# Powers in smaller pieces, two low parts and the phase tables later, and twelve rounds of transposes at other pairs, in a two-block transformer kernel

## The reference

```python
def first_block(x, ...):
    for layer in range(2):
        u_ssm, u_g, v_g, q, k, v = split(rms_norm(h, g) @ w_in[layer])
        mixed = concatenate([s5_mixer(u_ssm, ...), spatial_gating(u_g, v_g, ...), diff_attention(q, k, v, ...)])
        h = h + mixed @ w_out[layer]
        h = h + conv_gated_mlp(rms_norm(h, g2), w_up[layer], conv_w, conv_b, w_down[layer])   # 1024 -> 2 x 2816 -> 1024

def s5_mixer(u, ...):      # a complex diagonal state space model in 16 groups, 64 states each
    a_bar = exp(lam * dt); b_bar = ((a_bar - 1) / lam) * b
    states = associative_scan(...)            # s[t] = a_bar * s[t-1] + b_bar u[t]
    y = real(c @ states) + d_skip * u         # then GELU and a gated linear unit

def conv_gated_mlp(x, ...):
    h = x @ w_up
    acc = conv_b + conv_w[0] * h[t-2] + conv_w[1] * h[t-1] + conv_w[2] * h[t]
    gate, val = split(acc);  return (gelu(gate) * val) @ w_down

def second_block(x, mem, ...):
    a_qkv, bq, bk, bv, mq, ga, gb, gm, mg = split(rms_norm(x, g) @ w_in)
    # branch a: three dilated window attentions over rotated queries and keys
    # branch b: attention with normed, rotated heads; branch m: attention over 256 memory rows
    # the three branches are gated, projected, merged, projected and normed
```

## Time and profile before

| | us |
|---|---|
| Runs of the kernel | 999.23, 1001.0, 1001.94 (median 1001.0) |
| The profiled execution | 999.57 |
| Its span | 997.8 |
| TensorE busy | 966.1 |
| VectorE busy | 701.2 |
| ScalarE busy | 547.1 |
| GpSimd busy | 252.9 |

### The profile page before, as it was taken

One profiled execution on the slowest core, in us unless ns is written; L12 is line 12 of the kernel. 1 busy time (PEld: TensorE's weight loads), 2 busy tenths in 40 slices (PEclk: granted clock), 3 DMA queues, 4 the chain that ended last, 5 costly groups with the idle time before them and its releaser, 6 DMA issues.

```text
span 997.8 us, 15915 instructions
## 1 busy us (share of the span) xinstructions
PE 966.1 (97%) x6214; PEld 848.8 (85%) x6214; DVE 701.2 (70%) x1072; ACT 547.1 (55%) x898; POOL 252.9 (25%) x196
## 2 busy tenths in 40 slices
PE   6989999999999999999999999999999999999997
PEld 4868789999888887889999988999877789888886
DVE  6998557798954688657677856547676755666785
ACT  7645546665654655645576545545354454555723
POOL 4890102688400021102525300003112300000030
PEclk9999999999999999999999999999999999999999
DMA  7622355655565553247666664665544545754462
GB/s 295 213 84 85 88 186 178 189 179 177 172 188 166 168 171 127 64 138 232 190 191 189 188 192 149 205 209 177 169 148 148 148 142 158 218 152 156 148 190 85
DMA packets 48474, 165.97 MB, mean 166 GB/s; under 512 B 6544, under 2 KB 7056, under 8 KB 48400
## 3 DMA queue, kind: packets, MB, share of 16 engines
q1 hardware_dynamic: 48400, 164.95, 53.2%
HBM read 162.83 MB, written 1.05 MB: 164 GB/s over the span
## 4 chain that ended last, share of the span: by engine, by line
PE 81%; DVE 13%; ACT 2%; issue 2%; POOL 1%; DMA 1%; SPq 0%; DVEq 0%; POOLq 0%; ACTq 0%
PE PJ L583 13%; PE PJ L585 12%; PE PJ L584 12%; PE PJ L576 9%; PE PJ L577 9%; PE PJ L578 9%; DVE wlo L1670 5%; PE PJ L539 2%; PE PJ L541 2%; PE PJ L540 2%; DMA raw<-weights_in 1%; PE T L1013 1%; PE PJ L700 1%; PE T L1004 1%; ACT whi L1072 1%
## 5 line engine op out<-in xcount | busy, mean ns | idle before, releaser
L1670 DVE TENSOR_TENSOR wlo<-raw,whi 128x1024 fp32r<-128x1024 f32 x294 | 375.2, 1308 | 92.1 <-ACT whi L1072 89.8
L1072 ACT ACTIVATE whi<-raw 128x1024 fp32r<-128x1024 f32 x294 | 303.3, 1062 | 67.8 <-DMA raw<-weights_in 61.3
L576 PE MATMUL PJ<-xthb,whi 128*128 128x256 f32 x864 | 243.2, 281 | 4.5 <-DVE wlo L1670 3.7
L578 PE MATMUL PJ<-xthb,wlo 128*128 128x256 f32 x864 | 242.1, 280 | 0.0
L577 PE MATMUL PJ<-xtlb,whi 128*128 128x256 f32 x864 | 242.0, 280 | 0.0
L583 PE MATMUL PJ<-whi,xthb 128*128 128x512 f32 (+1 forms) x432 | 175.2, 406 | 5.7 <-DVE wlo L1670 3.6
L576 PEld LDWEIGHTS PJ<-xthb,whi 128*128 128x128 f32 x864 | 163.1, 189 | 6.4 <-issue 6.2
L585 PE MATMUL PJ<-whi,xtlb 128*128 128x512 f32 (+1 forms) x432 | 167.8, 388 | 0.0
L584 PE MATMUL PJ<-wlo,xthb 128*128 128x512 f32 (+1 forms) x432 | 167.8, 388 | 0.0
L577 PEld LDWEIGHTS PJ<-xtlb,whi 128*128 128x128 f32 x864 | 163.1, 189 | 0.2
L578 PEld LDWEIGHTS PJ<-xthb,wlo 128*128 128x128 f32 x864 | 163.1, 189 | 0.0
(11 more groups left out here) (398 smaller groups left out, 1382.9 us busy)
## 6 DMA issues: line engine op xcount, KB each, us to landing
raw<-weights_in SPq DMA_DIRECT2D x294, 512.0 KB, 3.5
rt<-bmerge_in SPq DMA_DIRECT2D x6, 256.0 KB, 4.4
xres<-x_in SPq DMA_DIRECT2D x2, 512.0 KB, 5.5
xn<-mem_in SPq DMA_DIRECT2D x2, 512.0 KB, 5.7
y_out<-xn SPq DMA_DIRECT2D x4, 256.0 KB, 2.4
rowv<-rows_in SPq DMA_DIRECT2D x1, 576.0 KB, 10.2
ptmp<-bexp_in SPq DMA_DIRECT2D x2, 256.0 KB, 6.1
cex<-cexp_in SPq DMA_DIRECT2D x2, 256.0 KB, 8.2
```

What stands on the lines that cost most here:

```text
L576: pe.matmul(o, a, xh[:, k, :], start=(first and f % 2 == 0), stop=False, skip_group_check=True)
L578: m = pe.matmul(o, b, xh[:, k, :], start=False, stop=last, skip_group_check=True)
L1072: act.activation(whi[:, p % HIGHS, :], raw[:, p % LOADS, :], ACT.Copy).then_inc(hi_ready, 1)
L1670: dve.tensor_tensor(wlo[:, p % LOADS, :], raw[:, p % LOADS, :], whi[:, p % HIGHS, :].bitcast(F32), ALU.subtract).then_inc(lo_ready, 1)
```

## The change

GpSimd's work for layer 1 is cut into smaller pieces and lies at j = 2 to 10 instead of 3 to 10. The two input powers are now two steps each at j = 2, 3 and 4, 5, the coefficients are at j = 6, the six products of the output powers at j = 7, 8 and 9 (two each), and the two copies and `gpow_ready` at j = 10. The turns (VectorE) and the tables (ScalarE) both move to the end of the loop, j = 11 = UNITS, behind unit 10's own low and high part. In layer 0 two low parts move from before `mix_low` to behind it. The rounds of branch a are taken out of pairs with n % 3 == 2: they were behind pairs 6, 7, 10, 11, 14, 15, 18, 19, 22, 23, 26, 27 and are now behind 6, 7, 10, 12, 15, 16, 18, 19, 22, 24, 27, 28.

```diff
+        ROTATED = []
+        for _c in range(1, 7):
+            for _t in range(TT):
+                _n = max(4 * _c + 2 + _t, ROTATED[-1] + 1 if ROTATED else 0)
+                ROTATED.append(_n + 1 if _n % 3 == 2 else _n)
...
-                    if 1 <= c <= 6 and j >= 2:
-
-                        t = j - 2
-                        rnd = 2 * (c - 1) + t
-                        pe.wait_ge(sem("a_rope"), 4 * c - 2 + 2 * t)
+                    if 4 * c + j in ROTATED:
+                        rnd = ROTATED.index(4 * c + j)
+                        t = rnd % TT
+                        pe.wait_ge(sem("a_rope"), 2 * rnd + 2)
...
-                    if l + 1 < LAYERS and j == UNITS - 1:
+                    if l + 1 < LAYERS and j == UNITS:
                         phase_tables(act, l + 1)
...
-                        if j in (3, 4):
+                        if j == 2:
                             pool.wait_ge(sem("bex_ready"), l + 2)
-                            input_powers(pool, link, l + 1, j - 3, x_tile(j - 3), ptmp)
-                        if j == 5:
+                        if 2 <= j < 6:
+                            input_powers(pool, link, l + 1, j // 2 - 1, x_tile(j // 2 - 1), ptmp, (j % 2,))
+                        if j == 6:
                             folded(l + 1)
-                        if j in (6, 7):
-                            output_powers(pool, link, l + 1, j - 6, ptmp)
+                        if j == 7:
+                            output_powers(pool, link, l + 1, 0, ptmp, (0, 1))
                         if j == 8:
+                            output_powers(pool, link, l + 1, 0, ptmp, (2,))
+                            output_powers(pool, link, l + 1, 1, ptmp, (0,))
+                        if j == 9:
+                            output_powers(pool, link, l + 1, 1, ptmp, (1, 2))
+                        if j == 10:
                             replicate_inputs(l + 1)
-                        if j == 10:
                             decay_table(pool, link, l + 1)
                             pool.sem_inc(sem("decay_ready"), 1)
...
-                lo_upto(s0 + 26)
+                lo_upto(s0 + (26 if l else 24))
                 mix_low(4, S1[:, :], 3)
                 mix_low(6, S0[:, :], 4)
...
-                    if l + 1 < LAYERS and j == 9:
+                    if l + 1 < LAYERS and j == UNITS:
                         dve.wait_ge(sem("gpow_ready"), 4)
                         phase_turns(dve, link, 1)
```

More of the change, by code:

```diff
@@ L379, in fold_coefficient, with output_powers @@
                 link(eng.tensor_tensor(o, o, t, ALU.add))
-        def output_powers(eng, link, l, c, tmp):
+        def output_powers(eng, link, l, c, tmp, steps=(0, 1, 2)):
             ar, ai = (wide(apw[:, c, 1:STEP + 1, 8 * l:8 * l + 8].rearrange("p t s -> p s t"), 32, 3) for c in range(2))
@@ L387, in output_powers, with input_powers @@
             o = gpw[:, c, :, 1:STEP + 1, :]
[L388 to L392, removed]
+            if 0 in steps:
+                link(eng.tensor_tensor(o, i0, k0, ALU.mult), False)
+            if 1 in steps:
+                link(eng.tensor_tensor(t, i1, k1, ALU.mult))
+            if 2 in steps:
+                link(eng.tensor_tensor(o, o, t, op))
+        def input_powers(eng, link, l, c, x, tmp, steps=(0, 1)):
             ar, ai = (wide(apw[:, k, 1:STEP, 8 * l:8 * l + 8].rearrange("p t s -> p s t"), 32, 3) for k in range(2))
@@ L399, in input_powers @@
             i1, k1, op = (bi, ai, ALU.subtract) if c == 0 else (br, ai, ALU.add)
[L400 to L404, removed]
+            if 0 in steps:
+                link(eng.tensor_copy(xv[:, :, 0, :], bex[:, c, :, :]), False)
+                link(eng.tensor_tensor(o, br if c == 0 else bi, ar, ALU.mult), False)
+            if 1 in steps:
+                link(eng.tensor_tensor(t, i1, k1, ALU.mult))
+                link(eng.tensor_tensor(o, o, t, op))
+                eng.sem_inc(sem("xpow_ready"), 1)
         @block.sync
@@ L1403, in _ @@
                             act.copy(va[:, g, t, :], PJ[buf(f"av{g}")][:, t, :]).then_inc(sem("av_ready"), 1)
-                    if 1 <= c <= 6 and j >= 2:
-                        rnd = 2 * (c - 1) + j - 2
+                    if n in ROTATED:
+                        rnd = ROTATED.index(n)
+                        t = rnd % TT
                         act.wait_ge(sem("a_tr"), rnd + 1)
-                        w, g = divmod(c - 1, NG)
-                        act.copy(aqT[:, w, g, :, P * (j - 2):P * (j - 1)], S1[:, :].rearrange("p (f n) -> p f n", f=4)).then_inc(sem("a_ev"), 1)
+                        w, g = divmod(rnd // TT, NG)
+                        act.copy(aqT[:, w, g, :, P * t:P * t + P], S1[:, :].rearrange("p (f n) -> p f n", f=4)).then_inc(sem("a_ev"), 1)
                     d = bm_slot(n, 1)
```

## The result

| | before | after |
|---|---|---|
| Median of twelve runs each, side by side | 999.88 | 1001.41 |
| Ratio, 95% interval | | 1.0017 (1.001 to 1.0024) |
| The profiled execution | 999.57 | 1000.13 |
| Its span | 997.8 | 998.3 |

The changed kernel is slower by 1.5 us. That is half of the 0.3% that the prediction gave as the limit of what can be told, but the interval of the ratio, 1.0 to 2.4 us, doesn't hold 1, so it is a real loss. Of the two profiled executions, after takes 0.56 us more. All ratios here are formed from runs measured side by side; they need not be the quotient of the two medians.

What follows compares the result with a forecast made beforehand. TensorE, busy 966.1 of 997.8 us, was taken to bound the kernel, so only its idle stretches count. The terms -3.4 + 2.5 + 2.5 - 1.4 - 0.2 = 0.0 were carried to the median 1001.0; range 997.3 to 1004.3.

Steps and rivals of the forecast that it cites:

- disturbance of units 7 to 10 gone: Layer 0 up-projection: GpSimd's spread powers stop taking turns with VectorE's low parts, so TensorE's lost time goes; -3.4 us.
- wait at the transposes of kmT: Behind unit 6, TensorE reaches kmT's transposes before GpSimd's later input powers are ready and restarts slower; +2.5 us.
- waits at down pairs 4 and 5: Layer 0 down-projection: low parts come late behind phase turns and tables that wait for GpSimd's copies; +2.5 us net.
- low parts of layer 0: Mixing of layer 0: with two low parts moved behind the mixing's own, TensorE's idle of 1.52 shrinks; -1.4 us.
- rotated rows: Attention: four of twelve transpose rounds move beside another piece, each costing 0.43 instead of 0.48; -0.2 us.
- rival 3: TensorE's clock falls behind both new waits, at kmT's transposes and the down-projection; +3.2 us, 1004.2, chance 0.15.
- GpSimd held off by a whole row: Unit 5: GpSimd's gate product gets in only behind VectorE's whole low-part row, taking 5.55 us; kmT ready at 220.4.
- Rival 1: Unit 5: GpSimd gets in behind one VectorE instruction, so no wait at kmT's transposes; 998.5 us, chance 0.12.
- nothing is left that takes turns with the low parts: Layer 0 up-projection: at most two wide GpSimd steps, 4.4 us, fit in the free 4.8 us behind each gate product.
- No low part group above 1.3 us an instruction: Expected profile sign for units 7 to 9 of the up-projection, together with sixteen pairs in about 44.9 us.
- The queue behind the turns: End of layer 0's up-projection: VectorE's wait for copies and phase turns holds eleven low parts; pair 4 waits 1.7 to 2.8.
- Rivals 2 and 4: Rival 2: neither consumer waits, -5.5, 995.5, chance 0.12. Rival 4: contention stays in units 8 and 9, 1003.2, chance 0.09.

Runs made afterwards that it cites:

- the powers alone: Changed kernel with layer 0's low parts and the rotated rows' rounds put back as before, only the powers moved; 1003.43 us, ratio to before 1.0033.
- the filled kernel: Changed kernel plus unused TensorE transposes, 20 before the wait for kmT and 24 before down pair 4; 1000.49 and 999.89 us, ratio to before 1.0005 both times.
- both repairs: Changed kernel with the sixteen transposes one unit later and down-projection parts taken ahead of phase tables and turns; 995.36 us, ratio to before 0.9948.

## Why the prediction was wrong, and what in it was right

As a change it was wrong: it said 0.0 us, and measured was +1.5 (1.0 to 2.4). That its time of 1001.0 lies 0.4 from the measured 1001.41 is in good part luck: the three runs of before that it was carried to had a median 1.1 above that of the twelve. From 999.88 the same sum gives 999.9.

Term by term, in the profiled execution:

| step | forecast | measured |
|---|---|---|
| disturbance of units 7 to 10 gone | -3.4 | -3.4 (48.24 to 44.88) |
| wait at the transposes of kmT | +2.5 | +2.36 (transposes 4.02 instead of 1.66) |
| waits at down pairs 4 and 5 | +2.5 | +2.0 at pair 4; +0.6 at pair 5 where the clock holds |
| low parts of layer 0 | -1.4 | -1.5 |
| rotated rows | -0.2 | -0.26 |
| clock falls | not in the sum; rival 3, chance 0.15, +3.2 | +1.6 at the transposes, +0.9 net at pair 4, each in about half of the profiles |

**The step that failed** is the last: the clock. The sum put it at nothing, and rival 3 made a fall behind both waits a case of its own with a chance of 0.15. The prediction's rows had a fall behind an idle of 3.15 and none behind one of 1.52; its two new waits, 2.4 and 1.7 to 2.8, lay between, where no row spoke. What the runs show: the profiles of this study have thirteen waits of 2.2 to 2.8 us at these two places, start to start, and the granted clock fell behind eight of them, four of six at the transposes and four of seven at pair 4. Length alone doesn't tell them apart: a wait of 2.74 brought a fall and one of 2.77 (the powers alone) didn't. With half a fall for each wait, 1.6 and 0.9 net, the forecast would have been 0.0 + 0.8 + 0.45, about +1.3, against +1.5 measured. That sum is made afterwards. What the falls weigh in time is shown by the filled kernel: 1.0005 in both measurements, which can't be told from no change, as the sum without falls had it, where the changed kernel has 1.0017, 1.0011 and 1.0020. These intervals overlap, so the share of the falls, 0.6 to 1.5 us, is known roughly.

**GpSimd held off by a whole row** (the ground under the end of unit 5's gate product) was right: 5.55 again, and kmT ready 2.4 late, as worked out. Rival 1, by which GpSimd gets in behind one instruction, fell at the transposes. But its mechanism shows in unit 7, against the statement that "nothing is left that takes turns with the low parts": there two low parts waited 0.20 and 0.24 for their high parts, the gate product slipped in at 238.15, and the two engines took turns. That cost TensorE nothing, so the term stood and its reason was too strong. "No low part group above 1.3 us an instruction" missed as well, for the same cause.

**The queue behind the turns** was right in mechanism and size: copies ended 2.4 behind the gate product (2.1 to 2.6 forecast), the turns took 2.2 (1.8 forecast), the wait was 2.36 (1.7 to 2.8), and the table load of 1.28 was hidden.

**Rivals 2 and 4** fell: both consumers waited, and units 8 and 9 were clean. Rival 2's price, -5.5 with neither wait, is close to what the kernel with both repairs gains (-5.2): the price was right, and this change didn't meet its condition. (That the times agree too, 995.5 and 995.36, is luck, by the start from 1001.0 again.)

## What to carry to other kernels

When producers are moved later, follow each consumer, and then what is queued behind the consumer's wait on its own engine: both waits here were of that kind, and two small moves of consumers turned +1.5 into -5.2 us. If the time doesn't improve when a semaphore is taken away, look whether the two engines now run in the same microseconds and stretch each other. And price a TensorE wait of the length seen here (2.2 to 2.8 us) at more than its length: add the fall of the clock behind it, with a chance, in the sum itself.

## What the runs showed of the chip that I had not expected

- The granted clock fell to half behind eight of thirteen idles of 2.2 to 2.8 us (start to start), for 3.4 us each, and behind five of the same lengths not. It fell right behind none of the twelve idles of 1.9 to 2.2 us at 57 us. The changed kernel has executions from 999.2 to 1003.75; such falls are a part of that spread.
- In layer 0, at 67 us, twelve of the fourteen profiles have a wait of 3.4 us (start to start). Where the clock fell right behind it, as in the earlier trace rows (seven profiles), the next wait, at 74, was 0.8 at most; where it didn't (five profiles), that wait was 2.2 and the clock fell behind it. What a fall costs and what it hides have to be read together, there as at pairs 4 and 5.
- VectorE's row of low parts held off a GpSimd instruction for the whole row (5.3 to 5.6 us for 1.2 of work, in every undisturbed unit). It got in where the row had a hole, of 0.24 us in unit 7 of after and of 0.11 in unit 8 with both repairs, and from then on the two alternated. It also got in without a hole where the low part ahead had itself just been held up by a GpSimd product: in unit 4 of the kernel before the gate product, issued at 200.10, took 1.87 us. The Trainium skill's rule ("SBUF — State Buffer", Who interferes with whom), an exclusive lock that whoever issues first holds for the whole instruction, covers the alternation (2.96 us for a product of 2.0 to 2.4, 2.5 for a low part of 1.2); that an undisturbed row without a hole counts like one instruction, only these rows show.
